# Two GpSimd operations per weight panel: 512 columns, then the rest, in a decoder step on one core

## Chip, core and metric

The kernel runs on one core of a Trainium2 chip. The metric is the device time of one execution in microseconds (us), the median of several runs. The core has TensorE (matmuls, PE in the rows), VectorE (DVE), ScalarE (ACT), GpSimd (POOL) and SyncE (SP, which here only issues transfers). They run side by side, wait for one another on semaphores, and share the on-chip memory SBUF. Matmul results land in PSUM (here the tensors `lin` and `px`).

## What is computed

One inference step of a two-layer decoder for 512 prompt tokens and 8 x 4 sample tokens, 544 token columns in all. Layer 0 is gated linear attention, layer 1 is multi-head latent attention over a paged cache; each is followed by a feed-forward part with a short convolution. Cut to what matters here, every weight enters through products of this kind:

```
def conv_ffn(h, buf, w_gate, w_up, conv_w, conv_b, w_down):
    T = h.shape[1]
    u = h @ w_gate
    upad = jnp.concatenate([buf.astype(u.dtype), u], axis=1)
    c = conv_b + sum(conv_w[j] * upad[:, j:j + T] for j in range(CONV_W))
    y = (jax.nn.gelu(c) * (h @ w_up)) @ w_down
    return y, upad[:, -(CONV_W - 1):]
```

The matrices are float32, and the result has to keep nearly that precision.

## The kernel before

**Three products for one.** A float32 matrix is split into a high part, rounded to the format that TensorE takes (fp32r), and a low part, what is left. Activations are split in the same way (`xg_h`, `xg_l`; in the feed-forward part also `xq_h`, `xq_l` and `a_h`, `a_l`). Each tile is the sum of high x high, low x high and high x low (`tile_matmuls`, L2272).

**Panels.** Weights come as panels of 128 rows by 1024, 1152 or 1408 columns (8, 9 or 11 chunks of 128 by 128), one output tile each. SP loads panel p into `w_raw[p % 2]`; ScalarE writes the high part into `w_h[p % 2]` (`split_hi` L837, in loops `split_hi_at` L844) and signals `w_hi`; GpSimd then writes the low part `w_l[p % 2]` = raw minus high (`split_lo` L711, in loops `split_lo_at` L716) and signals `w_lo`. TensorE waits for `w_lo` before the panel's first matmul (`take_panel`), and SP waits for `w_lo` of panel p - 2 before it loads panel p into the same slot. ScalarE begins the high part of p when TensorE is through with p - 2, so one panel is prepared while the panel ahead of it is being multiplied. The low parts of the first panel and of two late panels of the linear attention are made by VectorE (L1460).

**The order of the work** is written by hand for each engine. GpSimd runs the low parts of the panels in order; in the feed-forward parts (`ffn`) it also copies convolution state (L726, L727, L737, L757), subtracts partial results (L764, L765), and makes the low parts of quarter panels of 512 columns (`quarter_lo`, L732), for the 18 channel pairs of a layer whose products are formed from sums of quarters. In the attention over the cache it issues page transfers (L471).

**The entry of a feed-forward part.** Ahead of the 18 pairs come four plain channels (`PLAIN`). While TensorE multiplies their panels, VectorE has a long row of work: `xg_l` (L1449), the convolution and the gate product of the plain channels (L1740, L1742, L1784 and L1786 for the first of them), the normed input `xn` (L1808), its sums `xt` (L1816, L1818, L1821, L1824) and the low parts `xq_l` (L1832, L1835), which the first pair's products wait for (L2625). The entry exists twice, once in each layer.

**VectorE's operands.** Of VectorE's operations some read or write PSUM (`lin`, `px`), others have all operands in SBUF. Of the operations named above, L1449, L1784, L1786, L1816, L1818, L1821, L1824, L1832 and L1835 have SBUF operands alone; so have L1441 and L1444 (sums of squares), L1505 and L2012. L1844 and L1845 (sums of two quarters of a weight panel) read SBUF twice and write PSUM.

Of the kernel before, what the change touches and what calls it, by code (L numbers as in the profile page):

```python
# [16 lines left out]
F32 = mybir.dt.float32  # L17
# [3 lines left out]
ALU = mybir.AluOpType  # L21
# [63 lines left out]
def hi_parts(p):  # L85

    return p + (PRODUCTS - 1) * pairs_before(p)
# [37 lines left out]
def trunk_program(nc, io):  # L125
    ctx = ExitStack()
    with ctx:
        def sem(name):
            return ctx.enter_context(nc.semaphore(name))
# [12 lines left out]
        def keep(name, shape, dt=F32):  # L142
            off = pos[0]
            pos[0] += (4 * int(np.prod(shape[1:])) + 31) // 32 * 32
            return at(name, off, shape, dt)
# [3 lines left out]
        w_raw = keep("w_raw", [P, 2, SLOT])  # L149
        hi_off = pos[0]  # L150
        w_h = keep("w_h", [P, 2, SLOT], F32R)
        w_l = keep("w_l", [P, 2, SLOT], F32R)
# [146 lines left out]
        w_hi, w_lo = sem("w_hi"), sem("w_lo")  # L299
# [19 lines left out]
        def chunks_of(p):  # L319
            return 11 if P_F0B <= p < P_M1 or p >= P_F1B else 9 if P_UQ <= p < P_UK else 8  # L320

        def raw_panel(p):

            return flat(wq_raw[0][:]) if p in (P_F0B, P_F1B) else w_raw[:, p % 2, :]
# [377 lines left out]
        def _(pool):  # L702
            g = nc.gpsimd

            def split_lo(p):

                if p >= P_END:
                    return
                pool.wait_ge(w_hi, hi_parts(p + 1))
                n = P * chunks_of(p)  # L710
                g.tensor_tensor(w_l[:, p % 2, 0:n], raw_panel(p)[:, 0:n], w_h[:, p % 2, 0:n].bitcast(F32), ALU.subtract).then_inc(w_lo, 1)  # L711

            def split_lo_at(i, step_, p, chunks):
                pool.wait_ge(w_hi, i * step_ + hi_parts(p + 1))
                n = P * chunks
                g.tensor_tensor(w_l[:, p % 2, 0:n], w_raw[:, p % 2, 0:n], w_h[:, p % 2, 0:n].bitcast(F32), ALU.subtract).then_inc(w_lo, 1)  # L716

            def ffn(layer, pa, ta):
                f0, us0, ps_ = layer * FC, layer * US_ALL, pa + 2 * PLAIN
# [14 lines left out]
                for f in range(PLAIN):  # L734
                    if layer or f:
                        pool.wait_ge(c_done, f0 + f)
                    g.tensor_copy(u_pads, cs[:, f]).then_inc(us_done, 1)  # L737
                    if f != 1:
                        split_lo(pa + (3, None, 6, 7)[f])
                    if f:  # L740
                        pool.wait_ge(evac, ta + 2 * f + 1)
                    else:
                        pool.wait_ge(scaled, 4 * layer + 1)
                    buffer_out(f)
                    if f < 2:
                        split_lo(pa + 4 + f)
# [3 lines left out]
                def pair(i, j, last=False):  # L750

                    us1 = us0 + 3 * PLAIN
                    if i is None and j == 0:
                        quarter_lo(None, 0, 5, A12, 6)
                    ch = PLAIN + j if i is None else i * 2 + (PLAIN + j)
                    pool.wait_ge(c_done, count(i, f0 + PLAIN, 1, j))
                    g.tensor_copy(u_pads, cs[:, ch]).then_inc(us_done, 1)  # L757
                    if not last:
                        quarter_lo(i, j + 1, 0, A11, 1)
                    if last:  # L760
                        split_lo(P_F1B if layer else P_F0B)
                    pool.wait_ge(part_out, count(i, 4 * PAIRS * layer + 4, 4, j))
                    pool.wait_ge(us_done, count(i, us1 + 1, 5, j))
                    g.tensor_tensor(u[:, 2 + HALF:2 + SEQ], pt_d[:, 0:SEQ - HALF], pt_b[:, 0:SEQ - HALF], ALU.subtract).then_inc(us_done, 1)  # L764
                    g.tensor_tensor(u_new, by_sample(pt_d[:, SEQ - HALF:HALF], TS), by_sample(pt_b[:, SEQ - HALF:HALF], TS), ALU.subtract).then_inc(us_done, 1)  # L765
                    pool.wait_ge(us_done, count(i, us1 + 3, 5, j))
                    buffer_out(ch)
                    if not last:
                        quarter_lo(i, j + 1, 3, A22, 2 if i is None else 4)
                        quarter_lo(i, j + 1, 5, A12, 3 if i is None else 6)  # L770
# [9 lines left out]
            def ffn_down(pb):  # L780
                with pool.Fori(0, 7) as i:
                    for k in range(2):
                        split_lo_at(i, 2, pb + 2 + k, 11)
                split_lo(pb + 16)
                split_lo(pb + 17)
# [4 lines left out]
            with pool.Fori(0, (P_G2 - 3) // 2) as i:  # L790
                for k in range(2):
                    split_lo_at(i, 2, k + 3, 8)
# [2352 lines left out]
```

## Time and profile before

| | |
|---|---|
| median of 3 runs | 1475.28 us (1474.13 to 1475.62) |
| the profiled execution's own time | 1475.53 us |
| its span, first to last instruction | 1473.8 us |
| mean granted TensorE clock | 0.995 |
| TensorE busy | 1428.7 us (97%) |
| VectorE busy | 916.4 us (62%) |
| ScalarE busy | 676.6 us (46%) |
| GpSimd busy | 561.1 us (38%) |

Busy time is the time in which an engine had an instruction open, its waiting for a port of the memory included. The shares are averages over stages with different limits. What TensorE did not do is spread over some forty gaps of 0.1 us and more. A row of the timeline gives start and duration in us, then engine, line, operation, tensors and how many instructions were merged into it; in brackets the idle time of that engine before it, and what ended that.

### The profile page before, as it was taken

To read this page: it belongs to the slowest core of one execution; us is meant where nothing else is said; L and a number is where in the kernel's file an instruction comes from. 1 tells how busy PE (TensorE), PEld (TensorE's weight loads), DVE (VectorE), ACT (ScalarE), POOL (GpSimd) and SP (SyncE) were. 2 spreads that over 40 slices of the span, in tenths; PEclk is the share of its full clock that TensorE was granted. 3 is DMA by queue.
4 is the path that set the end of the run, shared out by engine and by line. 5 is a ranking of instruction groups with operands and counts; after the bars stand their busy time and mean duration, and the time that the engine had idled before them with its cause. 6 is when DMAs were issued, how large, how long until landed. Compare 5 with 4: busy or idle time off the path is not lost. (4 is left out here: it accounts for less than half of the span.)

```text
span 1473.8 us, 31036 instructions
## 1 busy us (share of the span) xinstructions
PE 1428.7 (97%) x11156; PEld 1304.1 (88%) x11156; DVE 916.4 (62%) x1506; ACT 676.6 (46%) x1281; POOL 561.1 (38%) x552
## 2 busy tenths in 40 slices
PE   6999999999999999999999999999999999999997
PEld 6999998988999999998986566666989999999997
DVE  4742446499999993236466744433579999995223
ACT  5433345375666672216313444443265565665211
POOL 1333111235555554341330044441315555554433
PEclk9999999999999999999999999999999999999999
DMA  4242322213232323222321099981212323223231
GB/s 165 72 144 86 115 86 101 91 58 104 97 103 96 103 88 112 97 79 96 104 81 33 4 283 287 280 261 46 102 47 87 115 85 114 85 84 109 82 98 66
DMA packets 56714, 160.19 MB, mean 109 GB/s; under 512 B 7633, under 2 KB 27602, under 8 KB 55330
## 3 DMA queue, kind: packets, MB, share of 16 engines
q1 hardware_dynamic: 50466, 137.82, 28.1%
q0 software_dynamic: 6144, 20.98, 4.6%
q8 instruction: 66, 1.08, 0.3%
q14 instruction: 38, 0.31, 0.1%
HBM read 150.72 MB, written 8.05 MB: 108 GB/s over the span
## 5 line engine op out<-in xcount | busy, mean ns | idle before, releaser
L716 POOL TENSOR_TENSOR w_l<-w_raw,w_h 128x1408 fp32r<-128x1408 f32 (+1 forms) x50 | 143.8, 2878 | 274.8 <-ACT w_h L837 153.3
L711 POOL TENSOR_TENSOR w_l<-w_raw,w_h 128x1024 fp32r<-128x1024 f32 (+2 forms) x42 | 108.1, 2575 | 284.1 <-ACT w_h L837 274.3
L2272 PE MATMUL lin<-xg_h,w_h 128*128 128x272 f32 x848 | 195.4, 303 | 17.1 <-DVE xg_l L1449 10.6
L2272 PE MATMUL lin<-xg_l,w_h 128*128 128x272 f32 x848 | 184.7, 290 | 0.0
L2272 PE MATMUL lin<-xg_h,w_l 128*128 128x272 f32 x848 | 184.6, 290 | 0.0
L2625 PE MATMUL lin<-xq_h,wq_r 128*128 128x272 f32 x864 | 170.1, 289 | 3.7 <-DVE xq_l L1835 3.6
L2625 PE MATMUL lin<-xq_h,w_h 128*128 128x272 f32 x576 | 166.3, 289 | 2.4 <-DVE xq_l L1835 2.3
L2625 PE MATMUL lin<-xq_h,w_l 128*128 128x272 f32 x576 | 166.0, 288 | 0.0
L2625 PE MATMUL lin<-xq_l,w_h 128*128 128x272 f32 x576 | 165.4, 287 | 0.0
L2272 PEld LDWEIGHTS lin<-xg_h,w_h 128*128 128x128 f32 x848 | 138.2, 191 | 25.0 <-issue 13.5
L837 ACT ACTIVATE w_h<-w_raw 128x1024 fp32r<-128x1024 f32 (+2 forms) x71 | 77.2, 1088 | 171.1 <-PE lin L2272 139.1
L2272 PE MATMUL lin<-a_h,w_h 128*128 128x272 f32 x704 | 154.1, 290 | 0.0
L2272 PE MATMUL lin<-a_l,w_h 128*128 128x272 f32 x704 | 152.5, 287 | 0.0
L2272 PE MATMUL lin<-a_h,w_l 128*128 128x272 f32 x704 | 152.3, 287 | 0.0
L2625 PEld LDWEIGHTS lin<-xq_h,wq_r 128*128 128x128 f32 x864 | 137.9, 188 | 4.9 <-ACT part L1131 2.7
L2272 PEld LDWEIGHTS lin<-xg_l,w_h 128*128 128x128 f32 x848 | 138.3, 191 | 0.3
L2272 PEld LDWEIGHTS lin<-xg_h,w_l 128*128 128x128 f32 x848 | 137.4, 190 | 0.0
L471 POOL DMA_DIRECT2D pages<-cache x128 | 68.8, 538 | 150.2 <-issue 143.3
L2625 PE MATMUL lin<-xq_l,wq_r 128*128 128x272 f32 x432 | 124.3, 288 | 0.0
L732 POOL TENSOR_TENSOR w_l<-wq_raw,w_h 128x512 fp32r<-128x512 f32 x72 | 108.9, 1513 | 23.7 <-ACT w_h L1123 23.6
L2272 PEld LDWEIGHTS lin<-a_l,w_h 128*128 128x128 f32 x704 | 113.6, 188 | 0.2
L2272 PEld LDWEIGHTS lin<-a_h,w_h 128*128 128x128 f32 x704 | 112.8, 188 | 0.2
(407 smaller groups left out, 3238.4 us busy)
## 6 DMA issues: line engine op xcount, KB each, us to landing
wq_raw<-w SPq DMA_DIRECT2D x38, 1024.0 KB, 5.0
w_raw<-w SPq DMA_DIRECT2D x61, 512.0 KB, 3.5
w_raw<-w SPq DMA_DIRECT2D x30, 704.0 KB, 4.1
pages<-cache SPq DMA_DIRECT2D x128, 160.0 KB, 3.8
pages<-cache POOLq DMA_DIRECT2D x128, 160.0 KB, 3.8
St<-state SPq DMA_DIRECT2D x4, 1024.0 KB, 6.0
gla_s<-St SPq DMA_DIRECT2D x4, 1024.0 KB, 3.9
w_raw<-w SPq DMA_DIRECT2D x4, 576.0 KB, 3.8
```

The lines of the kernel that those rows point to most:

```text
L471: eng.dma_start(pages[k][:, j * ROW:(j + 1) * ROW], io["cache"][page, :, cols]).then_inc(ready[k], 16)
L711: g.tensor_tensor(w_l[:, p % 2, 0:n], raw_panel(p)[:, 0:n], w_h[:, p % 2, 0:n].bitcast(F32), ALU.subtract).then_inc(w_lo, 1)
L716: g.tensor_tensor(w_l[:, p % 2, 0:n], w_raw[:, p % 2, 0:n], w_h[:, p % 2, 0:n].bitcast(F32), ALU.subtract).then_inc(w_lo, 1)
L732: g.tensor_tensor(wq_l[n], quarter(j, which), wq_h[n].bitcast(F32), ALU.subtract).then_inc(w_lo, 1)
L837: fn(w_h[:, p % 2, 0:n], raw_panel(p)[:, 0:n], ACT.Copy).then_inc(w_hi, 1)
L2272: last = mm(lin[:, 2 * out_set + half, 0:HALF], w[:, slot, (w0 + k) * P:(w0 + k + 1) * P], (v[ch] if isinstance(v, list) else v[:, ch, :]) ...
L2625: last = mm(lin[:, out, 0:HALF], w[n][:, k * P:(k + 1) * P], v[n][:, k, :], start=start and k == 0 and m == 0, stop=stop and k == 3 and m ...
```

## The change

The low part of a panel is made in two operations instead of one: first columns 0 to 511, then the rest (512, 640 or 896 columns). Both follow one wait for `w_hi`, and `w_lo` is signalled by the second. Nothing else differs: the quarter panels (L732) stay as they are, and so do all waits and counts. The order of the instructions of every engine is the same, apart from the second operation behind each first one.

```diff
             def split_lo(p):
@@
                 pool.wait_ge(w_hi, hi_parts(p + 1))
                 n = P * chunks_of(p)
-                g.tensor_tensor(w_l[:, p % 2, 0:n], raw_panel(p)[:, 0:n], w_h[:, p % 2, 0:n].bitcast(F32), ALU.subtract).then_inc(w_lo, 1)
+                for cols in (slice(0, 512), slice(512, n)):
+                    last = g.tensor_tensor(w_l[:, p % 2, cols], raw_panel(p)[:, cols], w_h[:, p % 2, cols].bitcast(F32), ALU.subtract)
+                last.then_inc(w_lo, 1)
 
             def split_lo_at(i, step_, p, chunks):
                 pool.wait_ge(w_hi, i * step_ + hi_parts(p + 1))
                 n = P * chunks
-                g.tensor_tensor(w_l[:, p % 2, 0:n], w_raw[:, p % 2, 0:n], w_h[:, p % 2, 0:n].bitcast(F32), ALU.subtract).then_inc(w_lo, 1)
+                for cols in (slice(0, 512), slice(512, n)):
+                    last = g.tensor_tensor(w_l[:, p % 2, cols], w_raw[:, p % 2, cols], w_h[:, p % 2, cols].bitcast(F32), ALU.subtract)
+                last.then_inc(w_lo, 1)
```

## Rows read from the trace of the kernel before

**Rows 1.** The page: costliest groups (busy us, mean ns | idle before), GpSimd's panel parts.

```profile
L716 POOL TENSOR_TENSOR w_l<-w_raw,w_h 128x1408 fp32r<-128x1408 f32 (+1 forms) x50 | 143.8, 2878 | 274.8 <-ACT w_h L837 153.3
L711 POOL TENSOR_TENSOR w_l<-w_raw,w_h 128x1024 fp32r<-128x1024 f32 (+2 forms) x42 | 108.1, 2575 | 284.1 <-ACT w_h L837 274.3
```

**Rows 2.** Waits of TensorE over the whole span (us in total, times, longest).

```profile
PE lin L2625 <- DVE xq_l L1835: 5.9, 6, 1.2
```

**Rows 3.** Timeline of TensorE: the four restarts that waited for a low part.

```profile
42.59 0.52 PE L2272 MATMUL lin<-xg_h,w_h 128*128 128x272 f32 x2 [0.80 <-POOL w_l L716]
...
250.46 0.52 PE L2272 MATMUL lin<-xg_h,w_h 128*128 128x272 f32 x2 [3.11 <-POOL w_l L711]
...
1020.87 0.39 PE L2272 MATMUL lin<-xg_h,w_h 128*128 128x272 f32 x1 [0.69 <-POOL w_l L711]
...
1039.37 0.52 PE L2272 MATMUL lin<-xg_h,w_h 128*128 128x272 f32 x2 [0.65 <-POOL w_l L711]
```

**Rows 4.** Timeline of GpSimd: two operations of 512 columns, back to back.

```profile
361.53 1.29 POOL L732 TENSOR_TENSOR wq_r<-wq_raw,wq_r 128x512 fp32r<-128x512 f32 x1
362.79 1.27 POOL L732 TENSOR_TENSOR w_l<-wq_raw,w_h 128x512 fp32r<-128x512 f32 x1
```

**Rows 5.** Timeline around 250 us: GpSimd's panel part and VectorE's copy.

```profile
248.07 2.34 POOL L711 TENSOR_TENSOR w_l<-w_raw,w_h 128x1024 fp32r<-128x1024 f32 x1 [30.90 <-ACT w_h L837]
...
248.50 2.21 DVE L1441 COPY ssq<-sq 128x544 f32<-128x544 f32 x1 [3.40 <-ACT sq L854]
```

**Rows 6.** Around 42 us: two panel parts in a row; VectorE's two L1505 (timeline, then line statistics).

```profile
40.19 4.87 POOL L716 TENSOR_TENSOR w_l<-w_raw,w_h 128x1024 fp32r<-128x1024 f32 x2 [9.25 <-ACT w_h L837]
...
41.36 3.98 DVE L1505 SCALAR_TENSOR_TENSOR g_q<-silr,eb 128x256 f32<-128x256 f32 x2
...
L1505 DVE SCALAR_TENSOR_TENSOR g_q<-silr,eb x8: 419/426/2597, 41.4 to 85.2; 128x256 f32<-128x256 f32 x8
```

**Rows 7.** Timeline around 1166 us: VectorE's two sums, GpSimd's quarter between them.

```profile
1165.62 0.71 DVE L1844 TENSOR_TENSOR px<-wq_raw 128x512 f32<-128x512 f32 x1
1166.24 1.78 DVE L1845 TENSOR_TENSOR px<-wq_raw 128x512 f32<-128x512 f32 x1
...
1165.73 1.74 POOL L732 TENSOR_TENSOR w_l<-wq_raw,w_h 128x512 fp32r<-128x512 f32 x1
```

**Rows 8.** Timeline of the first panel: GpSimd, VectorE, TensorE.

```profile
12.36 2.38 POOL L711 TENSOR_TENSOR w_l<-w_raw,w_h 128x1024 fp32r<-128x1024 f32 x1 [11.76 <-ACT w_h L837]
...
12.95 4.46 DVE L1449 SCALAR_TENSOR_TENSOR xg_l<-x,par,xg_h 128x544 fp32r<-128x544 f32 x4 [0.66 <-ACT xg_h L848]
...
21.43 1.18 PE L2398 MATMUL px<-ssq,ones 128*128 128x272 f32 x4 [0.49 <-DVE ssq L1444]
```

**Rows 9.** Timeline of the feed-forward entry of layer 0: GpSimd, then VectorE, then TensorE.

```profile
310.34 2.41 POOL L711 TENSOR_TENSOR w_l<-w_raw,w_h 128x1024 fp32r<-128x1024 f32 x1 [2.60 <-ACT w_h L837]
...
318.65 2.39 POOL L711 TENSOR_TENSOR w_l<-w_raw,w_h 128x1024 fp32r<-128x1024 f32 x1 [4.58 <-ACT w_h L837]
...
330.81 3.52 POOL L711 TENSOR_TENSOR w_l<-w_raw,w_h 128x1024 fp32r<-128x1024 f32 x1 [3.14 <-ACT w_h L837]
...
336.84 3.26 POOL L711 TENSOR_TENSOR w_l<-w_raw,w_h 128x1024 fp32r<-128x1024 f32 x1
...
312.32 3.79 DVE L1449 SCALAR_TENSOR_TENSOR xg_l<-x,par,xg_h 128x544 fp32r<-128x544 f32 x5
...
319.13 2.46 DVE L1784 TENSOR_TENSOR a<-a,gl 128x512 f32<-128x512 f32 x1
321.52 0.18 DVE L1786 TENSOR_TENSOR a<-a,gl 128x32 f32<-128x32 f32 x1
...
330.79 1.28 DVE L1818 TENSOR_TENSOR xt<-xn 128x1088 f32<-128x1088 f32 x1
...
339.27 1.98 DVE L1835 TENSOR_TENSOR xq_l<-xt,xq_h 128x1088 fp32r<-128x1088 f32 x1
...
353.32 0.36 PE L2625 MATMUL lin<-xq_h,wq_r 128*128 128x272 f32 x1 [1.15 <-DVE xq_l L1835]
```

## The prediction

> **What bounds the kernel.** I read the list of costliest groups first, for the operations that change: GpSimd makes 50 + 42 = 92 panel parts, each 2.4 to 3.2 us long, and stands idle before most of them until ScalarE has the high part [rows 1]. So GpSimd has time to spare, and TensorE, 97% busy, sets the pace. Then the waits of TensorE and its timeline, for the places where a later low part would cost something: of the 92 parts only four end a gap of TensorE, of 0.80, 3.11, 0.69 and 0.65 us [rows 3]. Third, the timelines of GpSimd and VectorE side by side, since operations of VectorE show durations far above their usual ones while a panel part runs.
>
> What the reader should see there: a copy of VectorE with all operands in SBUF starts 0.43 us after a panel part, and ends at 250.71, 0.30 us after the part's end at 250.41 [rows 5]. It was held for the whole part. L1784 ends at 321.59, 0.55 us after the part's end at 321.04 [rows 9]. It works the other way round too: a quarter that starts at 1165.73, behind L1844, ends at 1167.47, 1.14 us after L1844's end at 1166.33; and L1845, which asks after the quarter, is held until it is through, ending 0.55 us behind it [rows 7]. So whoever asks first goes first, and the other waits for the end of that one operation. All those held read tensors in SBUF alone. Two shorter GpSimd operations open a door in the middle; what this is worth depends on where VectorE is waited for. That is mainly the entry of each feed-forward part: VectorE works there without a pause, and TensorE waits for `xq_l` six times, 5.9 us in all over both layers [rows 2].
>
> **The change, part by part.**
>
> *The cost of a second operation.* Two of 512 columns back to back take from 361.53 to 364.06, 2.53 us [rows 4], one of 1024 takes 2.39 [rows 9]: +0.14, I take 0.15. Over 92 parts that is 14 us more of GpSimd, nearly all hidden: each part is made during the panel ahead, and GpSimd waited for ScalarE before it. If that cover were gone, all 14 us would show; with 558.9 us of idle time before the 92 parts [rows 1] it isn't. SP's next load into the slot waits for the same signal and is issued 0.15 us later, or 0.35 us where VectorE gets in; ScalarE takes up the new panel only when TensorE has left the one before, so nothing is queued behind it that TensorE waits for.
>
> *The four exposed low parts.* Here the added time is TensorE's. At 1020.87 no held operation of VectorE lies inside: +0.15. In the other three one of VectorE is waiting when the first half ends, and goes in between. For 250.46: first half 1.29 [rows 4], the copy's 0.30, then 1.14 for a half that has waited [rows 7], together 2.73 against 2.34: +0.39. At 1039.37 the same pair of operations meets, +0.35. At 42.59 it is L1505. That it gets in between two GpSimd operations is in the trace: the two parts there take 4.87 us instead of 4.78, of the two L1505 together 3.98 us one alone took 2.6, so the first ran in the gap between the parts and the second was held by the second part [rows 6]. +0.35 again. Sum: 0.15 + 0.39 + 0.35 + 0.35 = 1.2 us.
>
> *The first panel.* `xg_l` asks 0.59 us after the part [rows 8]. Now it runs from 13.65 instead of 14.74, but the second `xg_l` asks behind the second half and is held by it. The four took 2.67 us behind the part's 2.38, 0.67 each: 5.05 us; now 1.29 + 0.67 + 1.14 + 3 x 0.67 = 5.11. VectorE's row ends 0.06 us later, and TensorE, restarted a little earlier, waits for the squares' sum at 21.43 all the same [rows 8]. 0.1.
>
> *The feed-forward entries.* In order of time, layer 0 [rows 9]. (a) `xg_l` at 312.32 is held by the part that ends at 312.75; the door at 311.6 finds nobody waiting, so it is held 0.15 longer, and TensorE, which runs into it at 313.4, goes on 0.15 later. From here all times are 0.15 later. (b) L1784 gets in at the door 1.1 us early; but L1786 follows it directly, with SBUF operands alone, and asks later than the second half. It waits for that: 1.29 + 0.55 + 1.14 + 0.11 = 3.09 us against 2.39 + 0.55 + 0.11 = 3.05. The gain is given back, +0.04 for VectorE against TensorE. (c) At 330.8 L1818 asks 0.02 us ahead of the part and goes first; I take it that it still does. (d) The part of 336.84 ends at 340.10 and holds `xq_l` (339.27). The door opens at about 339.2, before `xq_l` asks: +0.15. VectorE is then 0.15 + 0.04 + 0.15 = 0.34 us late. Behind it GpSimd's quarters, ScalarE's parts and TensorE pull on each other; bounds are 0.15 (what TensorE had at (a)) and 0.34, and since `xq_l` is what TensorE waits for (1.15 us at 353.32), I take 0.3. Both layers: 0.6 us.
>
> *Other held operations.* In the feed-forward down part each `ssq` sum comes free sooner, and nobody waits for it there. A small remainder in the attention of layer 1, where VectorE's results end several short gaps, I put at 0.1, between 0 and 0.4.
>
> Sum: 1.2 + 0.1 + 0.6 + 0.1 = **+2.0 us**, on the profiled execution 1475.53 + 2.0 = 1477.5. That execution took 0.25 us more than the median of the runs shown, so I forecast 1475.28 + 2.0 = 1477.3 us, +0.14%. A measurement of this kernel can tell about 0.2%, 2.95 us, from no change; this is below.
>
> **A rule beside it.** The Trainium skill (SBUF — State Buffer, "SBUF: two separate sides") says that VectorE's second port pair is GpSimd's only one, and that the operation which starts first has it for the whole instruction while the other blocks. The traces agree [rows 5, 7].
>
> **The rivals.**
>
> *A, the order turns at 330.8: slower.* L1818 is ahead of the part by 0.02 us; by (b) it comes 0.04 us later. If GpSimd asks first, the first half holds L1818 for 1.14 us, in a row of VectorE without a pause, and all of it reaches `xq_l`. With a little more at (d), where the row is now later than the part, 1.15 to 1.45 us, say 1.3 per layer: 2.0 + 2 x 1.3 = +4.6, 1479.9 us. It decides at 0.02 us. For it: 0.04 is more than 0.02. Against it: where GpSimd wins in these rows it starts 0.43 us or more ahead [rows 5, 7, 9]; its start in the profile may lie before its claim, so that being ahead by 0.02 would not be enough. Chance 0.27.
>
> *B, the door is worth what it seems: no change or a little faster.* If L1786, only 32 columns, isn't held, VectorE keeps 1.1 us at (b), less 0.3 at (a) and (d): TensorE's wait at 353 shrinks by about 0.65 us in each layer. 1.2 + 0.2 - 1.3 = +0.1, 1475.4 us. Against it: no row shows a small operation pass a waiting GpSimd one, and the second L1505 was held [rows 6]. Further such gains in places that I hold for covered could reach the 5.9 us of [rows 2] only in part. Chance 0.16, a quarter of it beyond 0.2%.
>
> *C, the door doesn't open.* If GpSimd goes from half to half with no gap for VectorE, each held operation is held 0.15 longer; L1818 falls behind by 0.15, well past 0.02, and is held by both halves, 2.5 us. 4 x 0.15 + 0.2 + 0.1 + 2 x (0.3 + 2.4) = +6.3, 1481.6 us. Against it [rows 6], where the door opened between two panel parts; for it, that a wait for `w_hi`, already met, lay between those, and none does here. Chance 0.05. The Trainium skill (GPSIMD Engine Reference, "Instruction dispatch") says that each of GpSimd's cores starts the next instruction as soon as it has done its share of the one before; that rule speaks for C.
>
> **Numbers.** Forecast 0.52 (of it 0.07 over the bound), A 0.27, B 0.16, C 0.05. Faster by over 0.2%: 0.04. Slower by over 0.2%: 0.07 + 0.27 + 0.05 = 0.39. Within: 0.57. The range goes from 1474.6, a little below B, to 1481.0, A with its upper bounds. The likeliest case alone is 1476.3 to 1478.5.
>
> **What would show it.** GpSimd's idle gaps shrink and its busy time grows by about 14 us plus what VectorE takes inside. The copy at 248.5 lasts about 1.2 us instead of 2.21. The four gaps of [rows 3] are 0.15 to 0.4 us longer. L1784 lasts 1.4 us instead of 2.46, and L1786 1.3 instead of 0.18 (in B it stays at 0.18). L1818 lasts 1.28 (in A and C more, and it starts after GpSimd's part). The three gaps at 353 to 359 sum to 0.2 us more than before. I am wrong if L1818's duration changes, or if a door opens where VectorE's row, not TensorE, was the limit.

## The result, and where the time went

The changed kernel takes 1476.78 us, the median of 20 runs (1475.49 to 1478.11). The kernel before, run beside it, takes 1474.14 (20 runs, 1472.68 to 1475.68). The ratio is 1.0017, with a 95% interval of 1.0010 to 1.0024: 2.5 us slower, between 1.5 and 3.5. So the 0.2% that the prediction took as the smallest change to be told from none lies inside that interval, and with 20 runs each the slowdown is clear of zero. The profiled span grew from 1473.8 to 1476.0 us.

The page of the changed kernel first: its line of busy times, and the two groups of panel parts, which answer to [rows 1]. Line numbers have moved in this kernel: the two edited operations, L711 and L716, are L712 and L719, and all lines behind them are 4 further down (1784 became 1788, 1818 became 1822, 1835 became 1839).

```profile
PE 1430.1 (97%) x11156; PEld 1304.6 (88%) x11156; DVE 880.6 (60%) x1506; ACT 675.7 (46%) x1281; POOL 590.2 (40%) x646
...
L719 POOL TENSOR_TENSOR w_l<-w_raw,w_h 128x512 fp32r<-128x512 f32 x100 | 160.1, 1623 | 259.7 <-ACT w_h L841 146.5
L712 POOL TENSOR_TENSOR w_l<-w_raw,w_h 128x512 fp32r<-128x512 f32 x84 | 122.2, 1476 | 272.6 <-ACT w_h L841 262.9
```

The 92 parts are 184 operations now, with 282.3 us of busy time against 143.8 + 108.1 = 251.9. That is 30.4 us more. By the prediction's 0.15 us for each second operation 14 of it are theirs, and what is left, about 16, I put down to VectorE in the door between them. GpSimd still stands idle for 532 us before them, 27 less than before. VectorE's busy time went down by 36 us, from 916.4 to 880.6, because most of its held operations wait for half a part and not for a whole one: compared one by one in the two traces, 39 of them are shorter by more than 0.3 us, 53.9 us in all, and 14 are longer by more than that, 16.8 us in all. So the edit does what it says, on a large scale, and TensorE ends 2 us later. What TensorE waits for answers to [rows 2] (the waits of TensorE in the changed kernel: who is waited for, us in total, times, longest):

```profile
PE lin L2629 <- DVE xq_l L1839: 6.0, 6, 1.2
PE lin L2276 <- POOL w_l L712: 5.9, 5, 3.5
...
PE lin L2276 <- POOL w_l L719: 1.2, 1, 1.2
```

The 36 us that VectorE saved are not in the wait for `xq_l`, which is 0.1 us longer. The waits for low parts grew by 1.9 us, and there are six of them instead of four. These are TensorE's restarts in its timeline, in order (start, duration; in brackets the gap before and what ended it):

```profile
43.03 0.52 PE L2276 MATMUL lin<-xg_h,w_h 128*128 128x272 f32 x2 [1.16 <-POOL w_l L719]
...
251.26 0.52 PE L2276 MATMUL lin<-xg_h,w_h 128*128 128x272 f32 x2 [3.46 <-POOL w_l L712]
...
281.73 0.39 PE L2276 MATMUL lin<-xg_h,w_h 128*128 128x272 f32 x1 [0.43 <-POOL w_l L712]
...
354.98 0.36 PE L2629 MATMUL lin<-xq_h,wq_r 128*128 128x272 f32 x1 [1.23 <-DVE xq_l L1839]
...
357.37 0.36 PE L2629 MATMUL lin<-xq_h,wq_r 128*128 128x272 f32 x1 [0.65 <-DVE xq_l L1839]
...
360.25 0.36 PE L2629 MATMUL lin<-xq_h,w_h 128*128 128x272 f32 x1 [1.13 <-DVE xq_l L1839]
...
1021.89 0.39 PE L2276 MATMUL lin<-xg_h,w_h 128*128 128x272 f32 x1 [0.83 <-POOL w_l L712]
...
1040.75 0.52 PE L2276 MATMUL lin<-xg_h,w_h 128*128 128x272 f32 x2 [0.99 <-POOL w_l L712]
...
1069.45 0.40 PE L2276 MATMUL lin<-xg_h,w_h 128*128 128x272 f32 x1 [0.17 <-POOL w_l L712]
```

Subtracting the start of the same restart in the two traces gives a running balance of how late TensorE is. The granted clock dips at the same two places in both executions (0.83 over 40 to 50 us and over 250 to 260), so the two can be compared row by row. The first row has to be read with care: GpSimd's first part starts at 12.52 in the changed kernel and at 12.36 before, so this execution is 0.16 us late before the edit has done anything.

| place, time before | late by | of it new | what |
|---|---|---|---|
| 21.43, first panel | +0.09 | +0.09 | 0.16 of a later start, -0.07 for the first panel |
| 42.59 | +0.44 | +0.35 | exposed low part |
| 250.46 | +0.80 | +0.36 | exposed low part |
| 291.95 | +1.39 | +0.59 | the new wait at 281.73, where a covered low part is late |
| 358.60 | +1.65 | +0.26 | feed-forward entry, layer 0 |
| 725.57 | +0.71 | -0.94 | the gap of 0.87 at 696.03 is gone, the one at 725.57 is 0.09 shorter |
| 769.55 | +0.57 | -0.14 | gap of 1.00 is 0.86 |
| 1010.02 | +0.89 | +0.32 | attention over the cache; a gap of 0.27 at 857.74 with no releaser ("issue") |
| 1020.87 | +1.02 | +0.13 | exposed low part |
| 1039.37 | +1.38 | +0.36 | exposed low part |
| 1079.27 | +1.81 | +0.43 | the new wait at 1069.45, where a covered low part is late |
| 1145.94 | +2.08 | +0.27 | feed-forward entry, layer 1 |
| 1463.65 | +2.17 | +0.09 | the end |

Two kinds of row need a word. The new waits cost more than their gaps of 0.43 and 0.17. The profile has matmuls of 0.29 us start every 0.125 us, and a gap counts only from the end of the last one: TensorE takes up the panel of 281.73 at 280.34 before, so it is 1.39 us late there and had been 0.80 late, 0.59 more. The run that leaves these parts whole (below) takes 41.49 and 39.89 us for the two stretches (250.46 to 291.95 and 1039.37 to 1079.27), against 41.49 and 39.90 before and 42.08 and 40.33 in the changed kernel, so all of +0.59 and +0.43 is theirs. And the +0.32 before 1010.02 isn't shown to be the change's. From the restart of 769.55 to that of 1010.02 it is 240.47 us before and 240.79 in the changed kernel, but 240.52 in the run below that has every part in halves as well, and 240.71 and 241.16 in two runs whose parts are whole there.

The gap that went away is the one I had not looked into. The kernel before, around 696 us: GpSimd, VectorE, TensorE.

```profile
692.30 2.36 POOL L711 TENSOR_TENSOR w_l<-w_raw,w_h 128x1024 fp32r<-128x1024 f32 x1 [14.36 <-ACT w_h L837]
...
692.89 2.35 DVE L1449 SCALAR_TENSOR_TENSOR xs_l<-x,par,xs_h 128x544 fp32r<-128x544 f32 x1 [0.81 <-ACT xs_h L848]
695.17 1.34 DVE L1431 COPY ckf<-lin 128x544 f32<-128x544 f32 x2
...
696.03 4.36 PE L2342 MATMUL lin<-xf_a,w_raw 128*128 128x272 f32 x18 [0.87 <-DVE ckf L1431]
```

The same place in the changed kernel:

```profile
693.97 2.99 POOL L712 TENSOR_TENSOR w_l<-w_raw,w_h 128x512 fp32r<-128x512 f32 x2 [14.24 <-ACT w_h L841]
...
694.56 1.27 DVE L1453 SCALAR_TENSOR_TENSOR xs_l<-x,par,xs_h 128x544 fp32r<-128x544 f32 x1 [0.81 <-ACT xs_h L852]
695.95 0.72 DVE L1435 COPY ckf<-lin 128x544 f32<-128x544 f32 x1
```

Before, the part held `xs_l` for 2.35 us, and the copy queued behind it on VectorE, though it reads PSUM and needs no port, came so late that TensorE ran dry for its bank. In the changed kernel `xs_l` goes through the door, is done at 695.83, and the copy waits for its own data and starts at 695.95; TensorE has no gap there. Nothing that asks for the port follows `xs_l` at once. That is what makes this door worth its whole 1.1 us to VectorE, unlike the one at L1784.

### The profile page after: what moved, and what is told of

The parts are those of the page before. It is cut to its first block, busy times and chain, and to the rows that moved or that the text cites. A ratio compares the mean times of both kernels' runs of the same rounds, so it can differ in the third digit from the quotient of the medians.

```text
span 1476.0 us, 31130 instructions
## 1 busy us (share of the span) xinstructions
PE 1430.1 (97%) x11156; PEld 1304.6 (88%) x11156; DVE 880.6 (60%) x1506; ACT 675.7 (46%) x1281; POOL 590.2 (40%) x646
## 4 chain that ended last, share of the span: by engine, by line
PE 82%; DVE 8%; issue 4%; ACT 3%; POOL 2%; DMA 1%; SPq 0%; POOLq 0%; ACTq 0%; DVEq 0%
PE lin L2276 34%; PE lin L2629 25%; PE lin L2847 4%; PE lin L2346 3%; PE px L2888 2%; PE px L2925 2%; POOL w_l L712 1%; PE px L2402 1%; PE px L2835 1%; PE px L2892 1%; PE px L2855 1%; PE lin L2801 1%; PE px L2547 1%; DVE xq_l L1839 1%; ACT w_h L841 1%
## 5 line engine op out<-in xcount | busy, mean ns | idle before, releaser
L719 POOL TENSOR_TENSOR w_l<-w_raw,w_h 128x512 fp32r<-128x512 f32 x100 | 160.1, 1623 | 259.7 <-ACT w_h L841 146.5
L712 POOL TENSOR_TENSOR w_l<-w_raw,w_h 128x512 fp32r<-128x512 f32 x84 | 122.2, 1476 | 272.6 <-ACT w_h L841 262.9
```

Of the source, the lines that this page charges most:

```text
L712: last = g.tensor_tensor(w_l[:, p % 2, cols], raw_panel(p)[:, cols], w_h[:, p % 2, cols].bitcast(F32), ALU.subtract)
L719: last = g.tensor_tensor(w_l[:, p % 2, cols], w_raw[:, p % 2, cols], w_h[:, p % 2, cols].bitcast(F32), ALU.subtract)
```

## The entry, door by door

GpSimd and VectorE side by side in the changed kernel, at the copy of [rows 5] and in the feed-forward entry of [rows 9] (first the two rows at 248, then the entry's).

```profile
248.52 2.68 POOL L712 TENSOR_TENSOR w_l<-w_raw,w_h 128x512 fp32r<-128x512 f32 x2 [30.76 <-ACT w_h L841]
...
248.96 1.13 DVE L1445 COPY ssq<-sq 128x544 f32<-128x544 f32 x1 [3.41 <-ACT sq L858]
...
320.17 2.99 POOL L712 TENSOR_TENSOR w_l<-w_raw,w_h 128x512 fp32r<-128x512 f32 x2 [4.58 <-ACT w_h L841]
...
320.65 1.36 DVE L1788 TENSOR_TENSOR a<-a,gl 128x512 f32<-128x512 f32 x1
321.94 1.27 DVE L1790 TENSOR_TENSOR a<-a,gl 128x32 f32<-128x32 f32 x1
...
332.32 2.42 POOL L712 TENSOR_TENSOR w_l<-w_raw,w_h 128x512 fp32r<-128x512 f32 x1 [2.98 <-ACT w_h L841]
...
332.31 1.29 DVE L1822 TENSOR_TENSOR xt<-xn 128x1088 f32<-128x1088 f32 x1
...
338.35 3.41 POOL L712 TENSOR_TENSOR w_l<-w_raw,w_h 128x512 fp32r<-128x512 f32 x2
...
340.78 2.12 DVE L1839 TENSOR_TENSOR xq_l<-xt,xq_h 128x1088 fp32r<-128x1088 f32 x1
```

The copy lasts 1.13 us (2.21 before), the part around it 2.68 (2.34). L1784, now 1788, lasts 1.36 (2.46). L1786, now 1790, multiplies 32 columns and lasts 1.27 us (0.18): it started half a microsecond after the second half and was held by it. L1818, now 1822, starts 0.01 us ahead of the part, goes first and lasts 1.29 (1.28); the first half waits for it, 2.42 us. The Trainium skill (SBUF — State Buffer, "SBUF: two separate sides") says that the operation that starts first has the pair for its whole instruction and the other blocks fully; the trace agrees at each of these places, with 1.27 us for an operation that takes 0.18 alone.

## The experiments

Eight kernels. All are the kernel before with another list of places at which a panel part is cut; the helper reads it like this, and each experiment below shows only what it puts there; three of them put a small operation of VectorE beside it, and the one with all parts in halves cuts those of `split_lo_at` too. A part is named by its start in the trace before.

```
+            edges = [0] + cuts_of(p) + [n]
+            for a_, b_ in zip(edges, edges[1:]):
+                last = g.tensor_tensor(w_l[:, p % 2, a_:b_], raw_panel(p)[:, a_:b_], w_h[:, p % 2, a_:b_].bitcast(F32), ALU.subtract)
+            last.then_inc(w_lo, 1)
```

**Whole parts where TensorE waits for them.** Of the 42 parts of `split_lo`, the six behind the gaps at 250.46, 281.73, 1020.87 (two), 1039.37 and 1069.45 are whole, and the other 36 in halves. The 50 of `split_lo_at`, which serves the loops and the gap at 42.59, are left whole as before.

```
+def cuts_of(p):
+    return [] if p in (P_G2 + 2, P_F0A - 1, P_M3, P_M3 + 1, P_M3 + 2, P_F1A - 1) else [512]
```

> The changed kernel, but with one operation for the panels that TensorE was seen to wait for (those made at about 42, 248, 278, 1018, 1037 and 1065 us, and all others of the loop that the one at 42 belongs to, that is every split_lo_at panel). Theory (the added time stands where a low part is awaited, with a held VectorE operation in the middle of it): the four old gaps are back at 0.80, 3.11, 0.69 and 0.65 us, the two new ones of 0.43 and 0.17 us are gone, together 1.8 us less than the changed kernel, so about 0.8 us more than before or less. Rival (the added time comes from GpSimd's load as a whole): the gaps grow nearly as much, time stays within 0.5 us of the changed kernel.

Measured: 1474.97 us, ratio to the kernel before 1.0 (0.999 to 1.0009). The four gaps are back at 0.81, 3.11, 0.69 and 0.65, the two new ones are gone, the one at 696 stays away, the first at 353 is 1.21. So what the changed kernel loses lies for the most part in the low parts that TensorE waits for: with them whole the runs can't tell the kernel from the one before, though 36 parts still have a second operation. TensorE's last restart is at 1463.46, 0.19 us earlier than before and 2.36 earlier than in the changed kernel.

**One door.** Only the part of 692.30 in halves.

```
+def cuts_of(p):
+    return [512] if p == P_M1 + 1 else []
```

> The kernel before with one panel alone made in two operations, the one of about 692 us. Theory: VectorE's xs_l is held there by the whole operation and is late for the copy that frees a bank of PSUM; let in after 512 columns it lasts 1.27 us instead of 2.35, TensorE's gap of 0.87 us at 696 is gone and nothing else moves: 0.87 us less than before. Rival (the gap is the turnaround of two tiles that end together): the gap stays and the time is that of before.

Measured: 1473.33 us, ratio 0.9993 (0.9984 to 1.0002). The gap of 0.87 at 696 is gone, every other gap is as before, and TensorE's last restart is at 1463.05 instead of 1463.65 with a start that was 0.07 later. From 291.95 to 725.57 the trace gains 0.92 us; 0.24 of it is lost again in the attention over the cache, the stretch that differs between runs anyway. The trace shows the gain, and the runs cannot tell it from none.

**Three pieces.** At (b) of the prediction, in both layers, the door is opened twice: the first piece is 256 columns, so that L1784 gets in early, the second only 128, so that L1786, which asks behind it, is held for a short one. All other parts whole.

```
+def cuts_of(p):
+    return [256, 384] if p in (P_F0A - DIRECT + 4, P_F1A - DIRECT + 4) else []
```

> The kernel before, with the panel part of about 319 us (and its like in layer 1, about 1106 us) made in three operations of 256, 128 and 640 columns, all others whole. Theory (who asks first goes first, and waits only for the operation that is open): L1784 gets in after 256 columns, L1786 after 128 more, so L1784 lasts about 0.9 us instead of 2.46 and L1786 0.5 or less; VectorE's row is about 1.2 us earlier from there on, L1818 stays ahead of GpSimd, and TensorE's wait at 353 (1.15 us) is shorter by 0.8 to 1.15 in each layer: 1.6 to 2.3 us less than before. Rival (VectorE's row is bound by others there): the gap at 353 and the time stay.

Measured: 1470.08 us, ratio 0.997 (0.9957 to 0.9982), faster than both kernels. Its timelines at (b), and TensorE's at the entry's end:

```profile
317.36 3.13 POOL L716 TENSOR_TENSOR w_l<-w_raw,w_h 128x256 fp32r<-128x256 f32 x3 [4.59 <-ACT w_h L843]
...
317.84 0.80 DVE L1790 TENSOR_TENSOR a<-a,gl 128x512 f32<-128x512 f32 x1
318.57 0.45 DVE L1792 TENSOR_TENSOR a<-a,gl 128x32 f32<-128x32 f32 x1
...
354.33 0.36 PE L2631 MATMUL lin<-xq_h,w_h 128*128 128x272 f32 x1 [0.22 <-DVE xq_l L1841]
...
356.64 0.36 PE L2631 MATMUL lin<-xq_h,w_h 128*128 128x272 f32 x1 [0.57 <-DVE xq_l L1841]
```

From the start of L1784 (1790 here) to the end of L1786 (1792) it is 318.57 + 0.45 - 317.84 = 1.18 us, where the kernel before took 321.52 + 0.18 - 319.13 = 2.57. Over the stretch that the kernel before does from 291.95 to 725.57 TensorE takes 1.97 us less, and from 1079.27 to the last restart 1.97 less as well. That is 3.9 us, as in the medians (1470.08 against 1473.99), where 1.6 to 2.3 had been expected: the direction was right and the size too small by about half. The 1.4 us that VectorE gains here bring 1.97 for each layer: a gain at the head of a row without a pause is passed on, and later holds fall away (the `xq_l` of 339.27 lasts 1.49 instead of 1.98, since the part over it, at 335.45 here, is not itself held by VectorE any more and lasts 2.41 instead of 3.26).

**The changed kernel's own door there, alone.** The same two parts, cut at 512 as the change does it.

```
+def cuts_of(p):
+    return [512] if p in (P_F0A - DIRECT + 4, P_F1A - DIRECT + 4) else []
```

> The kernel before, with only the part that holds L1784 (318.65 in layer 0, its like in layer 1) in 512 columns and the rest, the cut of the change. Theory: L1784 lasts 1.36 and L1786 1.27 as in the changed kernel, the door's gain is taken back by the second half, and the waits for xq_l stay within 0.1 us of before (1.15, 0.66, 1.13 in each layer): before + 0.1 us. Rival (what made the three-piece run faster is a door anywhere, not its place): the waits shrink by 0.7 us or more in each layer, before - 1.5 us.

Measured: 1473.84 us, ratio 1.0 (0.9991 to 1.0009).

```profile
318.60 2.99 POOL L716 TENSOR_TENSOR w_l<-w_raw,w_h 128x512 fp32r<-128x512 f32 x2 [4.58 <-ACT w_h L843]
...
319.07 1.36 DVE L1790 TENSOR_TENSOR a<-a,gl 128x512 f32<-128x512 f32 x1
320.36 1.27 DVE L1792 TENSOR_TENSOR a<-a,gl 128x32 f32<-128x32 f32 x1
...
353.26 0.36 PE L2631 MATMUL lin<-xq_h,wq_r 128*128 128x272 f32 x1 [1.17 <-DVE xq_l L1841]
```

The pair takes 2.56 us (2.57 before), and the way from 291.95 to 358.60 is 66.63 (66.65 before). One door at this place is worth nothing, a door with a short piece behind it 1.97 us. What counts is how long the piece is behind which the next operation of VectorE has to wait. It also parts the entry's +0.26 of the changed kernel: nothing of it is (b). The two traces agree, by the starts of ScalarE's operations: at 301.38 the changed kernel is 1.38 us late, at 317.52, behind (a), 1.52, at 335.70, behind (b) and (c), still 1.51, and at 343.69, behind (d), 1.66. So (a) and (d) cost 0.14 and 0.15, where the prediction has 0.15 each.

**A later VectorE, first try.** Two memsets of two columns ahead of L1816, in a kernel with whole parts, to turn the order at 330.8.

```
                 normed_input(7)
+                v.memset(spare[:, 4 * layer:4 * layer + 2], 0.0)
+                v.memset(spare[:, 4 * layer + 2:4 * layer + 4], 0.0)
                 input_sum(0)
```

> The kernel before, with two tiny memsets (128 x 2, into spare memory) on VectorE ahead of the first sum xt (L1816), in both layers; they read and write nothing that is used. They make VectorE 0.1 to 0.2 us later at 330.8, where L1818 started 0.02 us ahead of GpSimd's panel part. Theory (the order of the starts decides): the part now goes first, L1818 is held by all of it, about 3.5 us instead of 1.28, and TensorE's waits at 353 grow by about 2.4 us in each layer: 4.5 to 5 us more than before. Rival (VectorE keeps the port while it has an operation lined up): L1818 stays at 1.28 and the time grows by 0.2 to 0.4.

Measured: 1474.02 us, ratio 1.0 (0.9991 to 1.0009), and the order did not turn. GpSimd and VectorE:

```profile
329.10 3.53 POOL L717 TENSOR_TENSOR w_l<-w_raw,w_h 128x1024 fp32r<-128x1024 f32 x1 [3.13 <-ACT w_h L844]
...
329.07 1.29 DVE L1825 TENSOR_TENSOR xt<-xn 128x1088 f32<-128x1088 f32 x1
```

The memsets start 0.01 us apart, L1816 0.07 us behind them, and they delay nothing that can be seen; VectorE is still ahead, by 0.03 us. Neither the theory nor the rival of the expectation was put to the test, and this decides nothing on rival A.

**A later VectorE, with a delay that counts.** A maximum over 256 columns, 0.41 us, takes the memsets' place; its result is not used. Once with whole parts, once with every part in halves as in the change.

```
                 normed_input(7)
+                v.reduce_max(spare[:, layer:layer + 1], x[:, 0, 0:256], AX.X)
                 input_sum(0)
```

> The kernel before, whole parts, with one small reduction of VectorE (256 columns, SBUF alone, its result is not used) put ahead of L1816 in each layer, so that L1818 asks about 0.25 us later and GpSimd's part of 330.8 starts first. Theory (the one that starts first goes first, for its whole operation): L1818 is held until GpSimd's 1024 columns (before: 1408 as drawn) are through, about 2.2 us, and lasts 3.4 us instead of 1.28; VectorE's row is 2.4 us late in each layer, the waits for xq_l grow by about that: before + 4.8 us. Rival (the order of the starts does not decide, or VectorE's row has slack here): L1818 lasts 1.3 and the time is before + 0.5 us or less.

> The changed kernel (each part in 512 columns and the rest) with the same reduction ahead of L1816. This is rival A of the prediction made on purpose. Theory: GpSimd's first half starts first and holds L1818 for about 1.05 us, L1818 then goes through the door and lasts 2.3 us instead of 1.29; each layer is 1.3 us later than in the changed kernel (0.25 + 1.05), so the changed kernel + 2.6, before + 5. If the door did not open for it, L1818 would last 3.5 us and the time be the changed kernel + 5.

With whole parts: 1479.01 us, ratio 1.0029 (1.0017 to 1.0041). GpSimd starts 0.18 us ahead, and L1818 (1825 here) waits for all of it:

```profile
329.16 2.52 POOL L717 TENSOR_TENSOR w_l<-w_raw,w_h 128x1024 fp32r<-128x1024 f32 x1 [3.13 <-ACT w_h L844]
...
329.34 3.49 DVE L1825 TENSOR_TENSOR xt<-xn 128x1088 f32<-128x1088 f32 x1
```

With halves: 1478.54 us, ratio 1.0027 (1.0016 to 1.0038), with L1818 as line 1828:

```profile
330.75 3.73 POOL L717 TENSOR_TENSOR w_l<-w_raw,w_h 128x512 fp32r<-128x512 f32 x2 [2.98 <-ACT w_h L847]
...
330.94 2.38 DVE L1828 TENSOR_TENSOR xt<-xn 128x1088 f32<-128x1088 f32 x1
```

The holds are 3.49 - 1.28 = 2.21 and 2.38 - 1.29 = 1.09 us. The way from 291.95 to 358.60 takes 69.02 us with whole parts (66.65 before: +2.37) and 68.21 with halves (66.91 in the changed kernel: +1.30). Both agree with what was expected of the theory, and so does the time with whole parts, 5.2 us above the kernel before. With halves it is 4.7 above it, where 5 had been expected. Of the 1.30 us in a layer 1.09 are the hold, and the other 0.2 the delay that the reduction puts in itself. So rival A, 4.6 us above the kernel before in the prediction, is about what would have come if VectorE had asked 0.2 us later. And the door does open for an operation that is waiting: 2.38 us, not 3.5.

**The two gains together.** Three pieces at the two parts of the entries, one door at 692.30, all else whole.

```
+def cuts_of(p):
+    if p in (P_F0A - DIRECT + 4, P_F1A - DIRECT + 4):
+        return [256, 384]
+    return [512] if p == P_M1 + 1 else []
```

> The three pieces (cuts at 256 and 384) at the same two parts, and the one door at 692.3 (cut at 512), all other parts whole. Theory: the two gains add: the entry waits 0.22, 0.56, 0.28 in both layers as in the three-piece run, and the gap of 0.87 us at 696.03 gone: 0.7 us less than the three-piece run, before - 4.5 us, ratio 0.997 or less. Rival (VectorE's later start in one place takes it back): no difference to the three-piece run.

Measured: 1469.12 us (5 runs, 1467.46 to 1470.63), ratio to the kernel before 0.9965 (0.9952 to 0.9979), the fastest of all. The interval overlaps that of the three pieces alone, 0.9957 to 0.9982, so the runs don't show that the gains add; the trace does. TensorE's wait for `xq_l` is 1.6 us in four waits, against 5.9 in six in [rows 2]:

```profile
PE lin L2633 <- DVE xq_l L1843: 1.6, 4, 0.6
```

and the gap at 696 is gone. By the restarts, 2 x 1.97 from the entries and 0.88 from the door: 4.8 us. The medians differ by 4.7 (1469.12 against 1473.80).

## Why the prediction held, point by point

The forecast was +2.0 us, 0.14%, and the runs give +0.17%, +2.17 in the traces. The sign, the mechanism and the size were right. The absolute 1477.3 was 0.5 too high, since the kernel before had a median of 1475.28 in the three runs that the forecast stood on and of 1474.14 in the 20 beside the changed kernel. Of the +2.17, 0.16 is a later start and 0.32 the stretch of attention that differs between runs; what the traces show as the change's own is about +1.7, and the runs allow 1.5 to 3.5. The terms:

- **The exposed low parts.** Forecast 0.15 + 0.39 + 0.35 + 0.35 = 1.2; the four gaps grew by 0.14, 0.35, 0.34 and 0.36. Right. What was missed is that there are two more: the part of 277.87 before and its like in layer 1, which I counted as covered, now make TensorE wait, and cost 0.59 and 0.43 us. The first ended at 280.27 before, 0.07 us ahead of TensorE's first matmul of the panel, and with a second operation and one of VectorE in the door it is 0.6 us longer (3.01 us against 2.40). So the step "nearly all hidden: each part is made during the panel ahead" failed at these two, for 1.0 us.
- **The first panel.** Forecast +0.1, measured -0.07: the +0.09 of the table starts from an execution that was 0.16 late. The run with whole parts where awaited has this part in halves too, starts it at 12.36 as the kernel before does, and is 0.07 us earlier at 21.43. The row of VectorE that was to grow from 5.05 to 5.11 us from the part's start shrank to 5.00.
- **The feed-forward entries.** Forecast 0.3 for each layer, measured 0.26 and 0.27, and the steps as described: (b) is given back, L1784 1.36, L1786 1.27 (forecast 1.4 and 1.3), confirmed by the run with that door alone; (c) L1818 stays ahead, at 1.29. I had said that the three gaps would sum to 0.2 more. They sum to 3.01 instead of 2.93, 0.08 more; half of the entry's loss comes earlier, at (a).
- **Other held operations.** This is the mis-sized term: "+0.1, between 0 and 0.4". What stands in its place is a balance: +0.59 and +0.43 at the two low parts above, -0.94 up to 725.57, nearly all of it the gap at 696, -0.14 at 769 and +0.09 up to the end, together +0.03, and the +0.32 of the attention that isn't shown to be the change's. Either way it lies in the term's range by luck: its parts are about ten times the term, of both signs, and one was a gain where I had allowed none. The place at 696 was in the "small remainder in the attention of layer 1", and the step that failed was to look only at who waits for a held operation. The profile shows no wait for `xs_l` there, but the copy queued behind it on VectorE is what frees TensorE's bank. It is also the last sign of being wrong that the prediction names, a door opening where VectorE's row was the limit, though it made the kernel faster there and not slower.

**Rival A** (the order turns at 330.8) did not happen, but by 0.01 us in the profile: before it was 0.02. Made on purpose it costs 1.30 us in layer 0 and 1.25 in layer 1, the reduction's own 0.2 included, against 1.3 in the prediction. Where exactly the order turns is open, but between narrow bounds: VectorE went first when it started 0.01 to 0.03 us ahead, in every trace that has the case. GpSimd needs far less than the 0.43 us that the prediction had from its rows. In the kernel before its quarter of 1227.13 starts 0.11 us ahead of L1844 and holds it:

```profile
1227.13 1.29 POOL L732 TENSOR_TENSOR w_l<-wq_raw,w_h 128x512 fp32r<-128x512 f32 x1
...
1227.24 1.73 DVE L1844 TENSOR_TENSOR px<-wq_raw 128x512 f32<-128x512 f32 x1
```

L1844 lasts 1.73 us there and 0.71 in [rows 7], where it goes first.

**Rival B** (L1786 is not held) is refuted by its 1.27 us. But the gain that B imagined exists, 1.97 us for each layer, and is reached when the piece in front of L1786 is short. I had written that further gains in places held for covered could reach TensorE's 5.9 us for `xq_l` "only in part"; with the cuts in the right place 4.3 of these 5.9 go, and TensorE ends 3.9 us earlier (it meets a new gap of 0.3 in each layer, for a part of ScalarE). **Rival C** (the door doesn't open) is refuted wherever an operation of VectorE was waiting. The Trainium skill (GPSIMD Engine Reference, "Instruction dispatch") says that a core goes on with the next instruction as soon as it is through with its share; whatever the cores do, the row at 248.96 shows a waiting VectorE operation through in 1.13 us, between two of GpSimd that follow directly.

What is left open is the stretch of attention over the cache: the gap of 0.27 us at 857.74 that no semaphore ended (the run with whole parts where awaited has one of 0.29 at 865.01 instead, and the run with the reduction and whole parts one of 0.57 at 858.25, which a transfer of cache pages ended). Its spread over the traces, 240.4 to 241.2 us, is as large as most single terms.

## What to carry to other kernels

An operation that is held by another engine's long one gained nothing from a door in the middle when the next operation behind it needed the port too (2.56 us for the pair against 2.57): look at the pair, and make the piece that the second one meets short (1.18 us). Cut only where the one let in is waited for (here 3 parts of 92, for -0.35%), and leave whole what TensorE waits for, since a cut there is paid in full (0.13 to 0.36 us each here). Ask the same of parts that end just in time: two that were covered before cost 0.59 and 0.43. And where a held operation has no waiter of its own, ask who waits for the one queued behind it.

## What was not expected of the hardware

Executions of the same kernel differ by up to 4.1 us (1472.09 to 1476.15 over the 48 runs of the kernel before that stand beside the experiments), more than this change is worth, and a part of it is TensorE's clock. In these rows (stretch, its length, busy time of TensorE, weight loads, VectorE, ScalarE, GpSimd, then the granted clock, the DMA share and GB/s) the kernel before stands first:

```profile
40.00:50.00 10.00, 9.20 (x56) 8.53 (x55) 7.88 (x13) 1.17 (x2) 4.87 (x2) 0.83 0.34 107
```

and the kernel with pieces and door, which is the same up to there:

```profile
40.00:50.00 10.00, 9.20 (x68) 8.53 (x68) 8.62 (x14) 2.53 (x3) 4.97 (x3) 1.00 0.32 107
```

Both had stood still for 0.80 us before 43. In the one the clock fell from 2.4 GHz to the lower level, 1.2 GHz, for a part of the 10 us, in the other it did not; TensorE goes from its restart there to the one at 131.17 in 88.58 and 87.05 us, 1.5 us apart. At 250 to 260, after a gap of 3.1 us, the same happens: 0.83 in the kernel before and 1.00 in the three-piece run, 1.5 us less up to 291.95, which is most of the reason why that run's span is 5.3 us shorter and its median only 3.9. A trace that is compared with another has to be compared stretch by stretch, with the clock beside it; the sums above use stretches in which it is 1.00 in both, or has dipped in both.
